# Masks of two block-masked attentions: from matmuls of their own to extra contraction rows of q and k

## The chip, the cores and the metric

The kernel runs on one NeuronCore of a Trainium2 chip. Its time is the device time of one execution in microseconds (us). Three runs of the kernel before gave 829.72, 831.28 and 831.41 us; the median is 831.28.

## What is computed

Two layers of a streaming encoder, on 256 tokens (four chunks of 64) of width 1024, all in float32:

```python
for l in range(2):
    u = rms_norm(x, g_mix_pre)
    qa, ka, va, cq, ckv, ga, gb = split(u @ w_in)        # 1024, 128, 128, 384, 288, 1024, 1024 columns
    # A: 16 query heads in 2 groups of 8, 2 key heads, 64 wide, rotary;
    #    a query of chunk c sees the keys of chunks c-1 and c; a learned sink in the softmax's sum
    y_a = swa_sink_attention(rope(qa), rope(ka), va, sinks)
    # B: 8 heads, 96 wide (64 + 32 rotary), from low-rank latents;
    #    a query of chunk c sees the keys of chunks 0 .. c
    y_b = mla_attention(q(rms_norm(cq) @ w_uq), kv(rms_norm(c_kv) @ w_ukv, k_pe))
    m = sigmoid(ga + b0) * (y_a @ w_oa) + sigmoid(gb + b1) * (y_b @ w_ob)
    x = x + rms_norm(m @ w_out)
    x = x + rms_norm(relu(rms_norm(x) @ w_mlp_in)**2 @ w_mlp_out)
```

Both masks are by whole chunks: a score outside the allowed chunks is set to -1e30 before the softmax.

## The kernel before

Each engine has a program of its own, written out by hand in order, and they meet at semaphores. Nothing is scheduled: an engine that waits holds up all that stands behind it. Tokens lie in two tiles of 128 (t = 0, 1).

*Weights.* A weight piece is loaded by SyncE (`raw`), cast on ScalarE to its high part (`hi`, L582, buffer `w_hi`) and subtracted on VectorE to its low part (`lo`, L853, `w_lo`). A product then takes three matmuls (high times high, low times high, high times low: L1166 to L1168). The activations, turned by TensorE (L1143, bank `tp`), are split in the same way (`s_hi` on ScalarE L605 or L602, `s_lo` on VectorE L883 or L880).

*Attention.* Queries and keys are float32 and are not split. They are turned by TensorE into `tp`, four blocks of 128 columns a fill, and copied by VectorE (`turned_copy`) into `qT_a`, `kT_a`, `qT_b`, `kT_b`. For A the two groups share the partitions: group 0 lies at partitions 0 to 63 and group 1 at 64 to 127 of `qT_a` and `kT_a`, and `q_of_group` writes the queries into `tok` with the two groups interleaved by head, so that a block of 128 columns holds a head of either group.

The scores are worked off in 18 quanta (`QUANTA`): four of A at t = 0 with four heads of 128 keys; eight of A at t = 1 with two heads of 192 keys; two of B at t = 0 with four heads of 128 keys; four of B at t = 1 with two heads of 256 keys. For each quantum `scores` (L1250) issues one float32 matmul a head, which the trace shows as two passes, and then one more matmul (L1251) with two stationary rows of ones (`chunk_of`) and two rows of 0 and -1e30 (`mask`), which adds the mask to all heads of the quantum in the score bank.

Step i of 20 on TensorE (L1343 on): the scores of quantum i, the turned probabilities of quantum i-2 (`turn_probs`), one piece of the gate or output product (12 matmuls of 512 columns), the values of quantum i-2 (`values`, L1282), then what `EXTRA` lists for this step: a fill of q, k or finished y. VectorE takes the row maxima of each quantum (L942), copies the turned blocks, and splits a weight piece; ScalarE takes the exponentials (L669).

*Start.* GpSimdE builds constants before the layers: the frequencies, the identity, then `chunk_of` and `mask` (L451 to L461, 12 memsets, most of 64 columns on one partition), then the cosine table (L466 to L468). The constants are done at 5.9 us of the profiled execution and the table at 7.1. Only then come its reciprocal roots of the sums of squares (`to_rstd`, L476 and L480; the first two from 19.66 to 21.5), for which VectorE waits before it scales the first projection (L1041). Meanwhile VectorE works out the angles (L822 to L837, one after the other, each waited for), ScalarE waits for them with the sines (L563), the first instruction of its program, and then turns to the first `s_hi` and `w_hi`.

## Time and profile before

| | |
|---|---|
| time, median of three runs | 831.28 us |
| the profiled execution | 827.3 us from its first to its last instruction; no separate time is listed for it, the median of the runs is 4.0 us above its span |
| PE busy | 803.6 us, 97% |
| DVE / ACT / POOL busy | 511.2 / 407.9 / 124.4 us |
| DMA | 132.35 MB, mean 160 GB/s |
| score matmuls (L1250) | 192 passes: 128 of A, 64 of B; 4% of the chain |
| mask matmuls (L1251) | 36 |

PE, DVE, ACT, POOL and SP are TensorE, VectorE, ScalarE, GpSimdE and SyncE; PEld is TensorE's weight load. A busy PE is not a PE at its peak: matmuls overlap, each row's duration holds its way through the array, so what a matmul costs is read from the distance between the starts of neighbours. A bracket at a row's end is the engine's idle time before it and who ended it.

### The profile page before, as it was taken

How to read it: one execution, taken by the hardware profiler on the slowest of the kernel's cores; microseconds unless marked ns; L12 is line 12 of the kernel's file. 1: busy time of each engine (PE TensorE's matmuls, PEld its weight loads, DVE VectorE, ACT ScalarE, POOL GpSimd, SP SyncE). 2: the span in 40 equal slices, each digit the busy share in tenths (PEclk: the TensorE clock that was granted, in tenths of full speed). 3: DMA queues.
4: the chain of work that ended last, by engine and by line, in shares of the span. 5: the costliest groups of instructions: out<-in, count | busy, mean ns of one | idle time of the engine just before them, and what ended most of it. 6: DMA issues, size and time to landing. Idle time of an engine off the chain costs nothing.

```text
span 827.3 us, 13460 instructions
## 1 busy us (share of the span) xinstructions
PE 803.6 (97%) x4613; PEld 696.0 (84%) x4613; DVE 511.2 (62%) x685; ACT 407.9 (49%) x747; POOL 124.4 (15%) x204
## 2 busy tenths in 40 slices
PE   6999999999999999999979999999999999999997
PEld 5987877888779999999869888788878899999995
DVE  5767666566785545554567777666666854555554
ACT  6756434444474444444466574434345644454452
POOL 2443000001231000000015420000031200000000
PEclk9999999999999999999989999999999999999999
DMA  7647422334646555556328382321436555565521
GB/s 236 237 167 266 154 82 72 103 105 150 204 131 226 172 185 183 175 200 191 98 56 284 138 304 93 102 93 62 153 113 213 184 191 175 194 194 172 192 102 51
DMA packets 68476, 132.35 MB, mean 160 GB/s; under 512 B 2842, under 2 KB 10564, under 8 KB 68164
## 3 DMA queue, kind: packets, MB, share of 16 engines
q1 hardware_dynamic: 68276, 131.12, 47.6%
q8 instruction: 30, 0.49, 0.2%
q10 hardware_dynamic: 144, 0.52, 0.2%
q14 instruction: 26, 0.21, 0.1%
HBM read 130.59 MB, written 1.05 MB: 159 GB/s over the span
## 4 chain that ended last, share of the span: by engine, by line
PE 91%; DVE 4%; ACT 2%; issue 2%; DMA 1%; SPq 0%; ACTq 0%; POOL 0%; DVEq 0%; POOLq 0%
PE acc L1166 17%; PE acc L1167 17%; PE acc L1168 17%; PE sc L1416 6%; PE sc L1415 6%; PE sc L1414 6%; PE tp L1143 5%; PE acc L1282 5%; PE sc L1250 4%; PE acc L1200 4%; DVE w_lo L853 1%; ACT s_hi L605 1%; PE sc L1166 1%; PE sc L1168 1%; PE sc L1167 1%
## 5 line engine op out<-in xcount | busy, mean ns | idle before, releaser
L853 DVE TENSOR_TENSOR w_lo<-raw,w_hi 128x1024 fp32r<-128x1024 f32 (+3 forms) x256 | 311.9, 1234 | 192.1 <-ACT w_hi L582 187.1
L582 ACT CAST w_hi<-raw 128x1024 fp32r<-128x1024 f32 (+3 forms) x256 | 252.3, 996 | 215.1 <-PE acc L1168 143.9
L1166 PE MATMUL acc<-w_hi,s_hi 128*128 128x512 f32 (+3 forms) x680 | 262.9, 387 | 3.7 <-DVE w_lo L853 3.7
L1167 PE MATMUL acc<-w_lo,s_hi 128*128 128x512 f32 (+3 forms) x680 | 257.5, 379 | 0.0
L1168 PE MATMUL acc<-w_hi,s_lo 128*128 128x512 f32 (+3 forms) x680 | 257.5, 379 | 0.0
L1166 PEld LDWEIGHTS acc<-w_hi,s_hi 128*128 128x128 f32 x680 | 127.9, 188 | 28.0 <-DVE w_lo L853 5.6
L1168 PEld LDWEIGHTS acc<-w_hi,s_lo 128*128 128x128 f32 x680 | 127.8, 188 | 23.9
L1167 PEld LDWEIGHTS acc<-w_lo,s_hi 128*128 128x128 f32 x680 | 128.1, 188 | 21.0
L1414 PE MATMUL sc<-s_hi,w_hi 128*128 128x256 f32 x448 | 126.9, 283 | 0.0
L1416 PE MATMUL sc<-s_hi,w_lo 128*128 128x256 f32 x448 | 126.8, 283 | 0.0
L1415 PE MATMUL sc<-s_lo,w_hi 128*128 128x256 f32 x448 | 126.8, 283 | 0.0
L1414 PEld LDWEIGHTS sc<-s_hi,w_hi 128*128 128x128 f32 x448 | 85.9, 192 | 0.7
L1415 PEld LDWEIGHTS sc<-s_lo,w_hi 128*128 128x128 f32 x448 | 85.9, 192 | 0.5
L1416 PEld LDWEIGHTS sc<-s_hi,w_lo 128*128 128x128 f32 x448 | 85.9, 192 | 0.0
L493 POOL TENSOR_TENSOR tok<-k_b 128x512 f32<-128x512 f32 x32 | 36.4, 1159 | 266.5 <-ACT k_b L650 266.5
L669 ACT ACTIVATE probs<-sc,neg_m 128x128 f32<-128x128 f32 (+2 forms) x96 | 37.6, 402 | 49.6 <-DVE neg_m L945 34.8
L537 POOL TENSOR_TENSOR tok<-gate_a,gate_b 128x512 f32<-128x512 f32 x8 | 14.1, 1782 | 261.0 <-DVE gate_b L993 261.0
L602 ACT ACTIVATE s_hi<-tp 128x512 fp32r<-128x512 f32 x24 | 13.7, 596 | 48.4 <-PE tp L1143 48.4
L942 DVE TENSOR_REDUCE row_max<-sc 128x2 f32<-128x384 f32 (+2 forms) x36 | 22.6, 627 | 13.3 <-PE sc L1251 13.3
L605 ACT ACTIVATE s_hi<-tp,gain 128x128 fp32r<-128x128 f32 x76 | 21.1, 379 | 17.0 <-PE tp L1143 15.0
L650 ACT ACTIVATE k_b<-sc 128x512 f32<-128x512 f32 x28 | 15.2, 595 | 25.7 <-PE sc L1416 25.7
L1200 PE MATMUL acc<-w_hi,s_hi 128*128 128x384 f32 (+1 forms) x64 | 19.7, 429 | 7.5 <-ACT w_hi L582 6.8
(143 smaller groups left out, 778.4 us busy)
## 6 DMA issues: line engine op xcount, KB each, us to landing
raw<-in_w_mlp_in SPq DMA_DIRECT2D x32, 1024.0 KB, 5.3
raw<-in_w_mlp_out SPq DMA_DIRECT2D x32, 1024.0 KB, 5.0
raw<-in_w_in SPq DMA_DIRECT2D x24, 1024.0 KB, 6.4
raw<-in_w_oa SPq DMA_DIRECT2D x8, 1024.0 KB, 5.0
raw<-in_w_out SPq DMA_DIRECT2D x8, 1024.0 KB, 5.0
raw<-in_w_ob SPq DMA_DIRECT2D x4, 1024.0 KB, 5.0
raw<-in_w_in SPq DMA_DIRECT2D x4, 768.0 KB, 4.6
raw<-in_w_in SPq DMA_DIRECT2D x4, 576.0 KB, 6.1
```

What stands on the lines that cost most here:

```text
L582: s.copy(split_view(w_hi, p), raw_view(p)).then_inc(hi_ready, 1)
L669: ins = s.activation(probs[:, i % 2, a * w + skip:(a + 1) * w], sc[i % 2][:, a * w + skip:(a + 1) * w], ACT.Exp, bias=neg_m[:, c + a:c + a ...
L853: v.tensor_tensor(split_view(w_lo, p), raw_view(p), split_view(w_hi, p).bitcast(F32), ALU.subtract)\
L1143: ins = nc.tensor.transpose(b[0:rows, i * P:(i + 1) * P], src, ident[:, :])
L1166: mm(banks[t][:, 0:N], h[:, kk, tk], wh[:, k, :], start=(start and k == 0), stop=False)
L1167: mm(banks[t][:, 0:N], h[:, kk, tk], wl[:, k, :], start=False, stop=False)
L1168: ins = mm(banks[t][:, 0:N], low[:, kk, tk], wh[:, k, :], start=False, stop=(stop and k == b - a - 1))
L1200: ins = mm(acc[t][:, 0:N], xs[:, 2 * i + k, t * P:(t + 1) * P], w[:, k, :], start=(first and i == 0 and k == 0), stop=(last and i == 3 and ...
L1282: ins = mm(y[:, (h + a) * 64:(h + a + 1) * 64], pt, vv, start=(b == 0), stop=(b == w // P - 1))
L1414: mm(out, wh[:, k, cols], s1_hi[:, kk, :], start=(i == 0 and k == 0 and f % 2 == 0), stop=False)
L1415: mm(out, wh[:, k, cols], s1_lo[:, kk, :], start=False, stop=False)
L1416: ins = mm(out, wl[:, k, cols], s1_hi[:, kk, :], start=False, stop=(i == 3 and k == 1 and f % 2 == 1))
```

## The change

The mask matmul and its two constant tiles are gone. The turned tiles get extra rows: `qT_a` and `kT_a` have 66 rows (64 and one for each of the tile's two chunks), `qT_b` and `kT_b` have 100 (96 and one for each of the four chunks). The extra rows of q say in ones which chunk a query is of; those of k hold -1e30 where a query of that chunk may not see the key. They are written once, before the layers, by GpSimdE: 15 instructions (`chunk_rows`), a memset and two affine selects for each of five regions. `qT_a` now holds one token tile and 16 heads, all at partitions 0 to 63, so a block of 128 columns that is turned holds two heads of one group, and the odd heads are copied from partitions 64 to 127 down to 0 to 63: a fill of q takes two copies of half the partitions, and the fill of k takes four (two groups, and the 192 keys of tile 1 are stored apart from the 128 of tile 0). `tok` holds the queries in their natural order. In `EXTRA` the fill `("qA", 1, 1)` moves from step 2 to step 3 and the fills of B are reordered (q before k), the last one going to step 11.

```diff
 SCALE_B = BQK ** -0.5
+NCHUNK = SEQ // CHUNK
+AK, BK = AD + P // CHUNK, BQK + NCHUNK
+A_KEYS = (slice(0, P), slice(CHUNK, SEQ))
+A_AT = (slice(0, P), slice(P, P + SEQ - CHUNK))
 NGAIN = KD + KD + KQ + KV
...
 NQ = len(QUANTA)
+CONST_STEPS = 15
 NSTEP = NQ + 2
...
-EXTRA = {1: [("qA", 1, 0)], 2: [("qA", 1, 1)],
-         3: [("kB", 0, 0)], 4: [("qB", 0, 0)], 5: [("kB", 0, 1)], 6: [("qB", 0, 1), ("y", 0)],
-         7: [("kB", 1, 0)], 8: [("qB", 1, 0), ("y", 1)], 9: [("kB", 1, 1)], 10: [("qB", 1, 1)],
+EXTRA = {1: [("qA", 1, 0)], 3: [("qA", 1, 1)],
+         4: [("qB", 0, 0)], 5: [("kB", 0, 0)], 6: [("qB", 0, 1), ("y", 0)], 7: [("kB", 0, 1)],
+         8: [("qB", 1, 0), ("y", 1)], 9: [("qB", 1, 1)], 10: [("kB", 1, 0)], 11: [("kB", 1, 1)],
          12: [("y", 2)], 15: [("y", 3)], 18: [("y", 4)]}
...
         v_b = sb("v_b", [P, TT, BH * BV])
-        qT_a = sb("qT_a", [P, AG, SEQ])
-        kT_a = sb("kT_a", [P, SEQ])
-        qT_b = sb("qT_b", [BQK, BH, SEQ])
-        kT_b = sb("kT_b", [BQK, BH, SEQ])
+        qT_a = sb("qT_a", [AK, AH, P])
+        kT_a = sb("kT_a", [AK, AKV, A_AT[1].stop])
+        qT_b = sb("qT_b", [BK, BH, SEQ])
+        kT_b = sb("kT_b", [BK, BH, SEQ])
         probs = sb("probs", [P, 2, COL])
...
         ident = sb("ident", [P, P])
-        chunk_of = sb("chunk_of", [P, P], F32R)
-        mask = sb("mask", [P, 3, 2 * P], F32R)
         pos_i = sb("pos_i", [P, TT], I32)
...
-            return tok[:, t, :].rearrange("p (h g d) -> p g h d", g=AKV, h=AG)[:, g, :, :]
+            return tok[:, t, g * COL:(g + 1) * COL].rearrange("p (h d) -> p h d", h=AG)
...
-            sel, mk = chunk_of[:, :].bitcast(F32), mask[:, :, :].bitcast(F32)
-            steps.link(g.memset(sel, 0.0))
-            steps.link(g.memset(mk, 0.0))
-            for half in range(2):
-                r = 2 * 32 * half
-                steps.link(g.memset(sel[r:r + 1, 0:CHUNK], 1.0))
-                steps.link(g.memset(sel[r + 32:r + 33, CHUNK:P], 1.0))
-
-                steps.link(g.memset(mk[r:r + 1, 0, CHUNK:P], NEG))
-                steps.link(g.memset(mk[r:r + 1, 1:3, P + CHUNK:2 * P], NEG))
-
-                g.memset(mk[r + 32:r + 33, 1, CHUNK:P], NEG).then_inc(consts_ready, 1)
-                pool.wait_ge(consts_ready, half + 1)
+            consts = Steps(pool, consts_ready)
+
+            def chunk_rows(view, low, high, inside, outside):
+
+                _, heads, n = view.shape
+                consts.link(g.memset(view, inside))
+                consts.link(g.affine_select(
+                    out=view, in_=view, compare_op=ALU.is_ge, fill=outside, base=-CHUNK * low,
+                    pattern=[[0, heads], [1, n]], channel_multiplier=-CHUNK))
+                consts.link(g.affine_select(
+                    out=view, in_=view, compare_op=ALU.is_ge, fill=outside, base=CHUNK * (high + 1) - 1,
+                    pattern=[[0, heads], [-1, n]], channel_multiplier=CHUNK))
+
+            chunk_rows(qT_a[AD:AK, :, :], 0, 0, 1.0, 0.0)
+            chunk_rows(qT_b[BQK:BK, :, :], 0, 0, 1.0, 0.0)
+            chunk_rows(kT_a[AD:AK, :, A_AT[0]], -1, 0, 0.0, NEG)
+            chunk_rows(kT_a[AD:AK, :, A_AT[1]], 0, 1, 0.0, NEG)
+            chunk_rows(kT_b[BQK:BK, :, :], 1 - NCHUNK, 0, 0.0, NEG)
+            assert consts.n == CONST_STEPS
...
                 if name[0] == "kA":
-                    ins = v.tensor_copy(kT_a[:, :], b[:, 0:SEQ])
+                    for g in range(AKV):
+                        for t in range(TT):
+                            ins = v.tensor_copy(kT_a[0:AD, g, A_AT[t]], b[g * AD:(g + 1) * AD, A_KEYS[t]])
                 elif name[0] == "qA":
-                    _, t, h = name
-                    ins = v.tensor_copy(qT_a[:, 4 * h:4 * h + 4, t * P:(t + 1) * P],
-                                        b[:, :].rearrange("p (h n) -> p h n", h=4))
+                    _, t, g = name
+                    for odd in range(2):
+                        ins = v.tensor_copy(qT_a[0:AD, g * AG + odd:(g + 1) * AG:2, :],
+                                            b[odd * AD:(odd + 1) * AD, :].rearrange("p (h n) -> p h n", h=AG // 2))
                 elif name[0] in ("qB", "kB"):
...
                     dst = qT_b if name[0] == "qB" else kT_b
-                    ins = v.tensor_copy(dst[:, 4 * h:4 * h + 4, t * P:(t + 1) * P],
+                    ins = v.tensor_copy(dst[0:BQK, 4 * h:4 * h + 4, t * P:(t + 1) * P],
                                         b[0:BQK, :].rearrange("p (h n) -> p h n", h=4))
...
                     pe.wait_ge(probs_ready, pos.count(NQ, i - 1))
-                r0, r1 = (64 * g, 64 * g + 64) if kind == "A" else (0, P)
-                which = 0 if t == 0 else (1 if kind == "A" else 2)
                 b = sc[i % 2]
-
-                k0 = w // P - 1 if kind == "B" else 0
-                nk = w // P - k0
-                view = b[:, :].rearrange("p (h k c) -> p h k c", h=n, c=P)[:, :, k0:, CHUNK:P]
-                mk = mask[r0:r1, which, 0:w].rearrange("p (k c) -> p k c", c=P)[:, k0:, CHUNK:P]\
-                    .unsqueeze(1).to_broadcast([r1 - r0, n, nk, CHUNK])
                 for a in range(n):
                     if kind == "A":
-                        q = qT_a[r0:r1, h + a, t * P:(t + 1) * P]
-                        k = kT_a[r0:r1, skip:w]
+                        q = qT_a[:, g * AG + h + a, :]
+                        k = kT_a[:, g, A_AT[t]]
                     else:
...
                         k = kT_b[:, h + a, 0:w]
-                    mm(b[:, a * w + skip:(a + 1) * w], q, k, start=(a == 0), stop=False)
-                mm(view, chunk_of[r0:r1, :], mk, start=False, stop=True).then_inc(scores_ready, 1)
+                    ins = mm(b[:, a * w + skip:(a + 1) * w], q, k, start=(a == 0), stop=(a == n - 1))
+                ins.then_inc(scores_ready, 1)
...
                     _, t, h = name
-                    blocks = [tok[:, t, (4 * h + a) * AKV * AD:(4 * h + a + 1) * AKV * AD] for a in range(4)]
+                    blocks = [tok[:, t, (4 * h + a) * 2 * AD:(4 * h + a + 1) * 2 * AD] for a in range(4)]
                 elif name[0] in ("qB", "kB"):
...
                 turned(pos, ("qA", 0, 1))
-                pe.wait_ge(consts_ready, 2)
+                pe.wait_ge(consts_ready, CONST_STEPS)
                 for i in range(NSTEP):
...
                     for name in EXTRA.get(i, []):
-                        if i in (1, 3):
+                        if i in (1, 4):
```

TensorE, step 4 of a layer: the fill before it, the scores of the first quantum of A at t = 1, the turned probabilities and the first product matmuls. Before:

```order
L1143 MATMUL tp<-ident,k_b 96x128 x4
L1233 REGISTER_ALU
L1250 MATMUL sc<-kT_a,qT_a 128x192 x2
L1251 MATMUL sc<-mask,chunk_of 128x4x64
L1143 MATMUL tp<-ident,probs 128x128 x4
L1157 REGISTER_ALU
L1306 ISA
L1166 MATMUL acc<-w_hi,s_hi 128x512
```

After:

```order
L1155 MATMUL tp<-ident,tok 128x128 x4
L1245 REGISTER_ALU
L1254 MATMUL sc<-kT_a,qT_a 128x192 x2
L1155 MATMUL tp<-ident,probs 128x128 x4
L1169 REGISTER_ALU
L1310 ISA
L1178 MATMUL acc<-w_hi,s_hi 128x512
```

The mask matmul has gone from between the scores and the turned probabilities, and another fill stands ahead.

GpSimdE, the end of the constants and the cosine table behind them. Before:

```order
L455 MEMSET chunk_of 1x64
L456 MEMSET chunk_of 1x64
L458 MEMSET mask 1x64
L459 MEMSET mask 1x2x64
L461 MEMSET mask 1x64
L466 TENSOR_TENSOR cost<-turns 128x64
L467 TENSOR_SCALAR cost<-cost 128x64
L468 TENSOR_SCALAR sint<-sint 128x2x32
```

After:

```order
L458 MEMSET kT_a 2x2x192
L459 AFFINE_SELECT kT_a<-kT_a 2x2x192
L462 AFFINE_SELECT kT_a<-kT_a 2x2x192
L458 MEMSET kT_b 4x2048
L459 AFFINE_SELECT kT_b<-kT_b 4x2048
L462 AFFINE_SELECT kT_b<-kT_b 4x2048
L475 TENSOR_TENSOR cost<-turns 128x64
L476 TENSOR_SCALAR cost<-cost 128x64
L477 TENSOR_SCALAR sint<-sint 128x2x32
```

Ahead of the first row shown stand six more memsets before the change, and nine more instructions after it (the same three for `qT_a` and for `qT_b` over 2048 columns, and for `kT_a` over 2x128). All fifteen stand ahead of the cosine table and of the roots.

VectorE, the copies of turned A blocks ahead of the first scores (`tp` is the bank, L1061 and L1073 the sinks). Before:

```order
L853 TENSOR_TENSOR w_lo<-raw,w_hi 128x512
L898 ISA
L901 COPY kT_a<-tp 128x256
L898 REGISTER_ALU
L904 COPY qT_a<-tp 128x4x128
L898 REGISTER_ALU
L904 COPY qT_a<-tp 128x4x128
L1060 ISA
L1061 TENSOR_SCALAR neg_sink<-sink_in 128x16
```

After:

```order
L862 TENSOR_TENSOR w_lo<-raw,w_hi 128x512
L907 ISA
L912 COPY kT_a<-tp 64x128
L912 COPY kT_a<-tp 64x192
L912 COPY kT_a<-tp 64x128
L912 COPY kT_a<-tp 64x192
L907 REGISTER_ALU
L916 COPY qT_a<-tp 64x4x128 x2
L907 REGISTER_ALU
L916 COPY qT_a<-tp 64x4x128 x2
L1072 ISA
L1073 TENSOR_SCALAR neg_sink<-sink_in 128x16
```

One copy of k has become four, and each copy of q two.

## Rows read from the trace of the kernel before

**Rows 1.** The page, part 4: the chain that ended last, by engine.
```profile
PE 91%; DVE 4%; ACT 2%; issue 2%; DMA 1%; SPq 0%; ACTq 0%; POOL 0%; DVEq 0%; POOLq 0%
```

**Rows 2.** Stretch of one layer's attention: busy us (count), granted clock, DMA share, GB/s.
```profile
70.00:180.00 110.00, 110.00 (x628) 91.26 (x627) 72.59 (x125) 52.85 (x143) 2.38 (x3) 1.00 0.39 130
```

**Rows 3.** PE timeline, quantum of A, t = 0: start us, us, instructions.
```profile
80.42 0.60 PE L1143 MATMUL tp<-ident,tok 128*128 128x128 f32 x4
80.94 1.16 PE L1250 MATMUL sc<-kT_a,qT_a 64*128 64x128 f32 x8
...
82.56 0.48 PE L1166 MATMUL acc<-w_hi,s_hi 128*128 128x512 f32 x1
```

**Rows 4.** PE timeline, quantum of B, t = 0.
```profile
147.04 0.61 PE L1143 MATMUL tp<-ident,tok 128*128 128x128 f32 x4
147.49 1.06 PE L1250 MATMUL sc<-kT_b,qT_b 96*128 96x128 f32 x8
148.30 0.36 PE L1251 MATMUL sc<-mask,chunk_of 128*128 128x256 f32 x1
148.50 0.60 PE L1143 MATMUL tp<-ident,probs 128*128 128x128 f32 x4
148.86 0.48 PE L1166 MATMUL acc<-w_hi,s_hi 128*128 128x512 f32 x1
```

**Rows 5.** PE timeline, quantum of A, t = 1.
```profile
92.08 0.60 PE L1143 MATMUL tp<-ident,k_b 128*96 128x128 f32 x4
...
93.98 0.48 PE L1166 MATMUL acc<-w_hi,s_hi 128*128 128x512 f32 x1
```

**Rows 6.** PE timeline, quantum of B, t = 1.
```profile
163.15 0.61 PE L1143 MATMUL tp<-ident,tok 128*128 128x128 f32 x4
163.59 1.03 PE L1250 MATMUL sc<-kT_b,qT_b 96*128 96x256 f32 x4
164.27 0.41 PE L1251 MATMUL sc<-mask,chunk_of 128*128 128x128 f32 x1
164.52 0.60 PE L1143 MATMUL tp<-ident,probs 128*128 128x128 f32 x4
164.88 0.48 PE L1166 MATMUL acc<-w_hi,s_hi 128*128 128x512 f32 x1
```

**Rows 7.** DVE groups by shape: busy us, mean ns, idle before.
```profile
L904 DVE COPY qT_a<-tp 128x512 f32<-128x512 f32 x8 | 5.5, 691 | 4.9 <-PE tp L1143 4.8
...
L901 DVE COPY kT_a<-tp 128x256 f32<-128x256 f32 x2 | 0.8, 424 | 0.9 <-PE tp L1143 0.9
```

**Rows 8.** POOL timeline, start of the program.
```profile
2.21 0.29 POOL L442 TENSOR_SCALAR_AFFINE_SELECT ident<-ident 128x128 f32<-128x128 f32 x1 [0.25 <-POOL ident L441]
...
3.05 0.74 POOL L452 MEMSET mask<- 128x768 f32 x1
3.85 0.14 POOL L455 MEMSET chunk_of<- 1x64 f32 x1
...
19.66 0.19 POOL L476 TENSOR_TENSOR var<-sums,norm_k 128x1 f32<-128x1 f32 x1 [12.59 <-ACT squares L612]
```

**Rows 9.** DVE timeline, start of the program.
```profile
3.14 0.71 DVE L824 TENSOR_SCALAR ang<-freq,pos_f 128x32 f32<-128x32 f32 x2
...
5.11 0.19 DVE L837 TENSOR_SCALAR ang<-ang 128x64 f32<-128x64 f32 x1
...
23.23 1.13 DVE L1041 TENSOR_SCALAR latent<-acc,rstd 128x384 f32<-128x384 f32 x2
```

**Rows 10.** ACT timeline, start of the program.
```profile
7.18 1.12 ACT L605 ACTIVATE s_hi<-tp,gain 128x128 fp32r<-128x128 f32 x4
...
11.91 1.56 ACT L582 CAST w_hi<-raw 128x768 fp32r<-128x768 f32 x2 [0.80 <-DMA raw<-in_w_in]
```

**Rows 11.** POOL timeline, rotation of the queries.
```profile
58.91 1.30 POOL L335 TENSOR_TENSOR gate_a<-tok,sint 128x512 f32<-128x512 f32 x1 [7.06 <-ACT tok L710]
```

**Rows 12.** DVE timeline, the same stretch.
```profile
59.01 1.75 DVE L336 TENSOR_TENSOR tok<-tok,cost 128x512 f32<-128x512 f32 x1
```

## The prediction

> **What bounds the kernel.** I read the chain that ended last first: TensorE holds 91% of it, and no other engine more than 4% [rows 1]. The stretch of the attention, where most of the change lies, says the same: TensorE is busy for all of 110 us at full clock, VectorE for 73, ScalarE for 53, GpSimdE for 2, and the DMA engines for 39% [rows 2]. So in this stretch a matmul that goes is worth the distance that it held between its neighbours' starts, and nobody else ends the waits. The same stretch comes once more in the second layer. The second place to read is the start of the program, before the layers: there TensorE has nothing to do yet, and a chain over GpSimdE, VectorE and ScalarE decides when it begins [rows 8 to 10].
>
> **TensorE: the quanta of the attention.** I compare passages from the first of the four turns ahead of the scores to the first product matmul behind them.
>
> A at t = 0: 80.42 to 82.56, 2.14 us [rows 3]. B at t = 0 has the same counts and columns, but its q and k fill 96 partitions instead of 64: 147.04 to 148.86, 1.82 us [rows 4]. The 0.32 between them is the price of 64-row operands among 128-row ones; the first part of it is seen ahead of the scores, where four turns hold 0.52 us in front of A and 0.45 in front of B. With 66 rows I take A to behave as B with its 96. The mask itself: in B the passes stand 0.11 apart (147.49 to 148.30, eight passes and 0.03), and from the last of them to the turned probabilities it is 0.03 + 0.20 = 0.23, where 0.11 would stand without the mask: 0.12. So A at t = 0 gives 0.32 + 0.12 = 0.44.
>
> A at t = 1: 92.08 to 93.98, 1.90 us [rows 5]. B at t = 1: 163.15 to 164.88, 1.73 us, with passes of 256 columns 0.217 apart (163.59 to 164.27, less 0.03, by three) [rows 6]. With 192 columns a pass would be 0.163, and four of them 0.22 less: 1.51. Difference 0.39. The mask of B at t = 1: 0.03 + 0.25 - 0.217 = 0.065. So A at t = 1 gives 0.455.
>
> The Trainium skill, page "TensorEngine Tiling (Array Packing)", Key Properties, says that a change of tiling mode drains TensorE, and counts a contraction of up to 64 as its own mode. By that rule the 66-row operands stay in the full mode, which is what the 0.52 against 0.45 points to; without the rule only the masks would go (rival C).
>
> Per layer: 4 x 0.44 + 8 x 0.455 + 2 x 0.12 + 4 x 0.065 = 5.9; two layers 11.8 us. The first two quanta of a layer have no turned probabilities behind them; I price them alike. The rest of the moved work has one answer: the same 64 turns of q and k are issued, a fill has gone from step 2 to 3 and one from 10 to 11, and nobody waits for them closely. The extra contraction rows cost no time of their own: B's passes with 96 rows and the turns with 128 (147.04 to 147.49, four) both stand 0.11 apart [rows 4].
>
> **VectorE: the copies.** 512 columns take 0.691, 256 take 0.424 [rows 7]: 1.04 ns a column and 0.16 fixed. A fill of q goes from 0.69 to two of 0.42, which overlap a little; VectorE is busy for two thirds of the attention [rows 2], which hides it. The fill of k goes from 0.42 to two of 0.29 and two of 0.36, 1.3 in sum. Here something waits: TensorE's third fill needs the bank that the k fill leaves, and VectorE sits idle for the k fill to come (0.9 in two [rows 7]), so what is added lies on the path. Between 0.5 (full overlap of the fixed parts) and 0.9; I take 0.7 a layer, 1.4 in both. Left on TensorE: 11.8 - 1.4 = 10.4 us gained.
>
> **GpSimdE: the constants.** This is paid once. A memset of 768 columns takes 0.74, of 64 columns 0.14: 0.85 ns a column, so 2048 columns take 1.84 us. An affine select of 128 columns takes 0.29 [rows 8]. With the fixed part of a GpSimdE instruction that reads (0.19 for one column [rows 8]) that is 0.82 ns a column and 1.9 us for 2048; with the memset's fixed part (0.09) it is 1.57 ns and 3.3 us. I take 1.9, since a select reads. Three memsets of 1.84, six selects of 1.9, six small instructions of together 2.5, and 15 gaps of 0.06 make 20.5 us, from 2.8 to 23.3, where the old constants ended at 5.9 (the kernel before, *Start*, which has the other ends that I use).
>
> Two paths wait behind that. *The roots.* The cosine table (1.1 us) and two roots (0.85 each) follow: 26.1. VectorE needed them at 23.23 [rows 9], so by this path alone the start is 2.8 us late. *The port.* In the trace a VectorE instruction that both reads and writes SBUF does not run beside one of GpSimdE. Its first two angle steps, 32 columns each, take 0.71 together and end at 3.85, just behind GpSimdE's mask memset, which ran from 3.05 to 3.79 [rows 8, 9]. At 59.01 a rotation step takes 1.75 while GpSimdE runs from 58.91 to 60.21 [rows 11, 12]. So it stands until the other's instruction is over, and with instructions of 1.9 instead of 0.14 every step of the angle chain can cost one of them. Seven steps in a row follow each other by semaphores. GpSimdE's next instruction started 0.06 after its memset had ended (3.79 to 3.85), when VectorE's held steps had only just ended, so I take GpSimdE to be first each time. The first steps end with the first memset at 4.6, the six others behind the next five large instructions and a small one: 14.8. They ended at 5.3 (5.11 + 0.19 [rows 9]): 9.5 us later, and ScalarE's first split of x, 1.9 behind them [rows 10], as well. It then no longer waits for its first weights (0.8 in [rows 10] and a little before): 8.6. Last, VectorE's splits of the first four weight pieces, which read and write SBUF too, meet the last three large instructions: one more of them, about 2. Together 10.6 us late, with which the roots are long ready. Nothing catches it up, since TensorE bounds what follows.
>
> The Trainium skill, "GPSIMD Engine Reference", Key points, says that GpSimdE shares its SBUF interfaces with VectorE, in conflict with instructions that have two SBUF inputs or run in a two-port mode; the angle steps in the trace have been seen to be held.
>
> **Sum.** The profiled execution: 827.3 - 10.4 + 10.6 = 827.5 us of span, with 4.0 around it as in the median of the runs before: 831.5 us against 831.28. No change that can be measured (a measurement tells 0.2%, 1.7 us).
>
> **Rivals.**
>
> *A, faster.* VectorE slips in between two of GpSimdE's instructions. The small steps ran among memsets of 0.14 with 0.19 each, without a sign of being held, and GpSimdE's lead at each meeting is some hundredths of a microsecond. If every second step slips in, the angles are ready at some 10.7 and the start is 5 to 7 late; if rows on two or four partitions hold no port at all, only the roots count, 2.8. I take 5.5: 831.3 - 10.4 + 5.5 = 826.4 us. Against it: the first two steps were plainly held.
>
> *B, slower.* The affine selects are slower than 1.9 us, by the column or by the row of heads in their pattern, which the one select of the trace doesn't show. With 3.3 the angles wait for four selects more dearly (5.6 us) and the splits for one (1.4): 17.6 late, 838.5 us; it decides from about 2.2 us on. With 2.6 it is 835.0. I take 836. Against it: fixed parts of reading instructions are 0.19 in the trace. The skill's "GPSIMD Engine Reference", section 3.1, gives 1.03 cycles an element for a light body and 1.8 for the best ordinary loop; as an estimate from its 1.2 GHz, the second makes 3.1 us and speaks for this rival.
>
> *C, the change doesn't do what it says for A's operands.* The 66 rows switch as dearly as the 64 did, and only the masks go: about 24 x 0.12 + 4 x 0.12 + 8 x 0.065 = 3.9, less 1.4. With the start: 831.3 - 2.5 + 10.6 = 839.4 us. Against it: the 96 rows of B, which are no full height either, show no such step.
>
> **How the numbers follow.** My forecast 0.37, A 0.34, B 0.25, C 0.04. The forecast's own range is 829 to 834 (its start between 8.5 and 13), of which 0.06 lies more than 0.2% below and 0.07 as far above. Faster: 0.34 + 0.06 = 0.40. Slower: 0.25 + 0.04 + 0.07 = 0.36. The same: 0.24. The range reaches into A to 824.5 (roots only would be 823.7) and into B to 838.
>
> **What the profile after would show.** Score passages of A of 1.7 us at t = 0 and 1.45 at t = 1 instead of 2.14 and 1.90, with 0.44 for the four turns ahead; if they stay at 2.0, C holds. The first attention stretch shorter by 5.9 and the wait for the k copies longer by 0.7. GpSimdE's nine long instructions of 1.9 each: if the selects take over 2.2, B. The last angle step at 14.8 and the first `s_hi` at 16.7: if they come at 11 or earlier, A. VectorE's first scaled projection near 34 instead of 23.2. I am wrong in the main thing if the start is not late at all.

## The result: 0.36% slower, and the profile after

| | before | after |
|---|---|---|
| median, six runs of each on one chip | 830.5 us (829.54 to 831.41) | 833.09 us (832.35 to 833.65) |
| ratio, 95% interval | | 1.0036 [1.0025, 1.0047] |
| span of the profiled execution | 827.3 us | 831.9 us |
| from the turn of k to the last turned y, either layer | 112.37, 112.35 us | 108.59, 108.60 us |
| start of the turn of k, first layer | 65.22 us | 77.44 us |

The time lies in the forecast's range, 1.6 us above the value. But the forecast was 0.2 us slower than before, no change that can be measured, and 0.36% is more than the 0.2% that I had called the least that a measurement tells: in kind this is the outcome "slower", to which I had given 0.36. The two lower lines are read from starts on TensorE (`tp<-ident,kv_a` is the turn of k; the last turned y lies in `latent`); they carry the whole story. The attention gained 3.77 us a layer where 5.2 were forecast, and the start lost 12.2 where 10.6 were forecast. What lies between the two stretches and behind the second is alike in these two profiles (296.61 and 296.55; 240.73 in both).

The chain that ended last, by engine; it answers to [rows 1]:

```profile
PE 88%; DVE 7%; issue 2%; ACT 2%; DMA 0%; ACTq 0%; DVEq 0%; POOL 0%; POOLq 0%
```

VectorE has gone from 4 to 7%. Twelve microseconds later in the program than [rows 2], the stretch of the attention:

```profile
82.00:192.00 110.00, 109.34 (x634) 92.83 (x633) 78.29 (x135) 54.30 (x145) 3.58 (x2) 1.00 0.40 132
```

TensorE is no longer busy without a gap, and VectorE is busy for 78 us instead of 73. GpSimdE's start, which answers to [rows 8]:

```profile
2.85 1.80 POOL L458 MEMSET qT_a<- 2x2048 f32 x1
4.72 2.00 POOL L459 TENSOR_SCALAR_AFFINE_SELECT qT_a<-qT_a 2x2048 f32<-2x2048 f32 x1
6.79 2.00 POOL L462 TENSOR_SCALAR_AFFINE_SELECT qT_a<-qT_a 2x2048 f32<-2x2048 f32 x1
8.85 1.80 POOL L458 MEMSET qT_b<- 4x2048 f32 x1
...
22.03 2.47 POOL L462 TENSOR_SCALAR_AFFINE_SELECT kT_b<-kT_b 4x2048 f32<-4x2048 f32 x1
```

Memsets of 1.80 and, but for the last, selects of 1.94 to 2.00, as forecast (1.84, 1.9). VectorE beside them, against [rows 9]:

```profile
3.02 1.66 DVE L831 CAST pos_f<-pos_i 128x2 f32<-128x2 int32 x1 [3.02 <-DMA pos_i<-in_positions]
4.71 2.19 DVE L833 TENSOR_SCALAR ang<-freq,pos_f 128x32 f32<-128x32 f32 x2
6.94 1.91 DVE L841 TENSOR_SCALAR turns<-ang 128x64 f32<-128x64 f32 x1
8.88 1.82 DVE L842 TENSOR_SCALAR turns<-turns 128x64 f32<-128x64 f32 x1
10.74 4.27 DVE L844 SCALAR_TENSOR_TENSOR ang<-turns,ang 128x64 f32<-128x64 f32 x3
15.04 0.19 DVE L846 TENSOR_SCALAR ang<-ang 128x64 f32<-128x64 f32 x1
```

Compare the ends: 4.68 against GpSimdE's 4.65, 8.85 against 8.79, 10.70 against 10.65. Six of the nine steps end 0.03 to 0.08 us behind the long one beside them. The other three are short and were not held: the second one of L833 (0.23, in the gap that began at 6.72), the last one of L844 (0.22, beside a memset of 0.30) and L846. The angles are ready at 15.2 (forecast 14.8), the first scaled projection comes at 35.48 (forecast near 34).

Not every meeting holds VectorE, though. Its first split of a weight piece, with two inputs in SBUF, took its ordinary 0.96 beside a memset, and its second 1.95, held by the select that had begun at 19.94:

```profile
17.99 1.80 POOL L458 MEMSET kT_b<- 4x2048 f32 x1
18.98 0.96 DVE L862 TENSOR_TENSOR w_lo<-raw,w_hi 128x768 fp32r<-128x768 f32 x1 [3.08 <-ACT w_hi L591]
```

On TensorE a quantum of A at t = 0, one of A at t = 1 and one of B at t = 0 (of the last two the first and last line), against [rows 3 to 5]:

```profile
93.11 0.60 PE L1155 MATMUL tp<-ident,tok 128*128 128x128 f32 x4
93.55 1.06 PE L1254 MATMUL sc<-kT_a,qT_a 66*128 66x128 f32 x8
94.44 0.60 PE L1155 MATMUL tp<-ident,probs 128*128 128x128 f32 x4
94.80 0.48 PE L1178 MATMUL acc<-w_hi,s_hi 128*128 128x512 f32 x1
...
103.47 0.61 PE L1155 MATMUL tp<-ident,tok 128*128 128x128 f32 x4
...
104.93 0.48 PE L1178 MATMUL acc<-w_hi,s_hi 128*128 128x512 f32 x1
...
155.75 0.61 PE L1155 MATMUL tp<-ident,tok 128*128 128x128 f32 x4
...
157.44 0.48 PE L1178 MATMUL acc<-w_hi,s_hi 128*128 128x512 f32 x1
```

A at t = 0 holds 1.69 us (it was 2.14), A at t = 1 holds 1.46 (1.90), B at t = 0 holds 1.69 (1.82): 0.45, 0.44 and 0.13 less, as forecast, and 0.44 stands ahead of the scores of A. So TensorE was handed its gain. Who took it back stands in the waits of TensorE from just ahead of the turn of k to the end of the first layer's attention (who waited for whom, us in total, times, longest), before and then after:

```profile
PE acc L1166 <- DVE w_lo L853: 1.3, 1, 1.3
```

```profile
PE acc L1178 <- DVE w_lo L862: 1.5, 2, 1.3
PE tp L1155 <- DVE kT_a L912: 0.8, 1, 0.8
PE acc L1286 <- DVE probsT L932: 0.5, 1, 0.5
```

All of them are VectorE's. The wait of 1.3 falls ahead of the turn of k in both (its matmul starts at 64.07 before) and is outside the stretch; the other 1.5 us of the kernel after are new. VectorE's rows at the first fills and in step 4:

```profile
77.86 1.13 DVE L912 COPY kT_a<-tp 64x128 f32<-64x128 f32 x4 [0.43 <-PE tp L1155]
79.02 2.81 DVE L916 COPY qT_a<-tp 64x512 f32<-64x512 f32 x4
...
105.47 1.38 DVE L916 COPY qT_a<-tp 64x512 f32<-64x512 f32 x2
106.89 0.56 DVE L954 TENSOR_REDUCE row_max<-sc 128x2 f32<-128x384 f32 x1
...
107.65 0.69 DVE L932 COPY probsT<-tp 128x512 f32<-128x512 f32 x1
```

A q copy of 64 partitions has 512 columns and takes 0.69, exactly what one of 128 partitions took [rows 7]. I had put 0.42. Four of them stand ahead of the weight piece that the first score step multiplies with, and two in step 4 stand ahead of the row maxima and of `probsT`, for which the values wait (the 0.5 above).

### The profile page after: what moved, and what is told of

Read it like the earlier page. It is cut to its first block, busy times and chain, and to the rows that moved or that the text cites. A ratio compares the mean times of both kernels' runs of the same rounds, so it can differ in the third digit from the quotient of the medians.

```text
span 831.9 us, 13410 instructions
## 1 busy us (share of the span) xinstructions
PE 795.3 (96%) x4577; PEld 693.2 (83%) x4577; DVE 526.2 (63%) x699; ACT 407.3 (49%) x747; POOL 145.2 (17%) x207
## 4 chain that ended last, share of the span: by engine, by line
PE 88%; DVE 7%; issue 2%; ACT 2%; DMA 0%; ACTq 0%; DVEq 0%; POOL 0%; POOLq 0%
PE acc L1178 17%; PE acc L1180 16%; PE acc L1179 16%; PE sc L1420 6%; PE sc L1419 6%; PE sc L1418 6%; PE acc L1286 5%; PE tp L1155 4%; PE acc L1212 4%; PE sc L1254 3%; DVE w_lo L862 2%; ACT s_hi L614 1%; PE sc L1178 1%; PE sc L1180 1%; PE sc L1179 1%
## 5 line engine op out<-in xcount | busy, mean ns | idle before, releaser
L1178 PEld LDWEIGHTS acc<-w_hi,s_hi 128*128 128x128 f32 x680 | 127.9, 188 | 29.1 <-DVE w_lo L862 5.6
L546 POOL TENSOR_TENSOR tok<-gate_a,gate_b 128x512 f32<-128x512 f32 x8 | 14.1, 1782 | 251.7 <-DVE gate_b L1005 251.7
L1212 PEld LDWEIGHTS acc<-w_hi,s_hi 128*128 128x128 f32 x64 | 12.9, 221 | 22.9 <-ACT w_hi L591 19.5
L954 DVE TENSOR_REDUCE row_max<-sc 128x2 f32<-128x384 f32 (+2 forms) x36 | 22.6, 627 | 11.6 <-PE sc L1254 11.4
```

What stands on the lines that cost most here:

```text
L1178: mm(banks[t][:, 0:N], h[:, kk, tk], wh[:, k, :], start=(start and k == 0), stop=False)
L1212: ins = mm(acc[t][:, 0:N], xs[:, 2 * i + k, t * P:(t + 1) * P], w[:, k, :], start=(first and i == 0 and k == 0), stop=(last and i == 3 and ...
```

## The experiments

Each was timed in five rounds beside the kernel before, in three sessions, where the median of before was 830.17, 830.15 and 830.88 us. All times are medians; all carry a ratio to before of the same session with its interval. "The stretch" is the one from the turn of k to the last turned y, 112.37 before and 108.59 after.

### The constants alone

```diff
+            chunk_rows(qT_b[BQK:BQK + 2, :, :].rearrange("p h (c n) -> p (h c) n", n=P), 0, 0, 1.0, 0.0)
+            chunk_rows(qT_b[BQK:BK, :, :], 0, 0, 1.0, 0.0)
+            chunk_rows(qT_b[BQK:BQK + 2, 0:2, 0:P], -1, 0, 0.0, NEG)
+            chunk_rows(qT_b[BQK:BQK + 2, 0:2, 0:192], 0, 1, 0.0, NEG)
+            chunk_rows(kT_b[BQK:BK, :, :], 1 - NCHUNK, 0, 0.0, NEG)
```

> The kernel before, with one thing added: the 15 instructions of chunk_rows on GpSimdE, of the same shapes, behind the old mask constants, into rows that nobody reads. Nothing in the attention changes. Theory (VectorE is held, each of its steps for one whole instruction of GpSimdE, even if that writes two or four partitions): the angles are ready near 15 to 16, the first s_hi near 17 to 18, VectorE's first scaled projection near 35 to 36, and the kernel is 12 to 13 us slower than before, 843. Rival (rows on so few partitions hold nobody, only the roots behind the constants come late): 2.8 to 4 us slower, 834. Second rival (the start is caught up later, behind a TensorE that had slack): under 2 us.

Measured: 840.58 us, 1.0122 [1.0107, 1.0137], 10.4 slower. The size is near the theory's 12 to 13, the way is not. Written behind the old mask constants, the long instructions came too late to meet the angle chain:

```profile
5.20 0.20 DVE L860 TENSOR_SCALAR ang<-ang 128x64 f32<-128x64 f32 x1
...
15.54 4.51 DVE L876 TENSOR_TENSOR w_lo<-raw,w_hi 128x768 fp32r<-128x768 f32 x2
...
32.42 1.14 DVE L1064 TENSOR_SCALAR latent<-acc,rstd 128x384 f32<-128x384 f32 x2 [4.99 <-POOL rstd L503]
```

```profile
6.05 1.80 POOL L473 MEMSET qT_b<- 2x2048 f32 x1
...
10.00 2.73 POOL L477 TENSOR_SCALAR_AFFINE_SELECT qT_b<-qT_b 2x2048 f32<-2x2048 f32 x1
...
30.66 0.19 POOL L499 TENSOR_TENSOR var<-sums,norm_k 128x1 f32<-128x1 f32 x1 [0.25 <-POOL sint L491]
```

The angles were done at 5.4, then VectorE's splits were held instead (two took 4.51, where they took 1.81), GpSimdE's selects were held in turn (2.73 instead of 2.0), and the roots came 11 us late (30.66 against 19.66), so VectorE waited 4.99 for them. The holding goes both ways. The clock adds to it: TensorE stood idle for 6 us behind the late roots, and the stretch after that reads a granted clock of 0.50 (the figure behind the counts), where its passes of 288 columns stood 0.24 apart instead of 0.13:

```profile
34.80:41.50 6.70, 5.88 (x26) 5.89 (x27) 4.08 (x7) 3.02 (x9) 2.46 (x5) 0.50 0.69 229
```

From the first scaled projection to the turn of k it took 44.2 us here and 42.0 before. So some 2.2 of the 11.4 us by which the start is late came by a way that the kernel after doesn't have, and that the sum is near 12 is luck.

So I moved the same instructions ahead of the old constants, where the change has them.

> The kernel before, with the 15 long GpSimdE instructions of the change ahead of its old mask constants, at the place in the program where the change has them; nobody reads what they write. In the run with them behind the old ones VectorE's angle steps had all slipped by before the first long one began (the last at 5.20, the first long memset at 6.05), and only the roots came late (31.2). Theory: now the angle chain meets them as in the kernel after: angles at 15, first s_hi at 17 to 18, and the whole is 12 to 14 us slower than before (the old constants and the table come on top): 843. Rival (the start costs what the roots cost, in whichever order): 10.4 again, 840.6.

Measured: 841.1 us, 1.0132 [1.0115, 1.0149], 10.95 slower. Its angle steps are those of the kernel after to 0.02 us; the last one (15.04 there):

```profile
15.05 0.20 DVE L861 TENSOR_SCALAR ang<-ang 128x64 f32<-128x64 f32 x1
```

The turn of k stands at 76.63, the stretch is 112.38. The expected whole was 843. By the time alone the rival's 840.6 is nearer; the trace decides for the theory, since here the angle chain is held and no roots are waited for, as in the kernel after. Its span is 12.1 us longer than before's, its median only 10.95; the difference is treated under "Span and median" below. The constants alone cost 11 us, and nothing of it is caught up.

### The constants behind the cosine table

```diff
-            chunk_rows(qT_a[AD:AK, :, :], 0, 0, 1.0, 0.0)
-            chunk_rows(qT_b[BQK:BK, :, :], 0, 0, 1.0, 0.0)
...
             g.tensor_scalar(sint[:, :, 0, :], sint[:, :, 1, :], -1.0, None, ALU.mult).then_inc(tables_ready, 1)
             pool.wait_ge(tables_ready, 1)
+            chunk_rows(qT_a[AD:AK, :, :], 0, 0, 1.0, 0.0)
+            chunk_rows(qT_b[BQK:BK, :, :], 0, 0, 1.0, 0.0)
...
```

> The kernel after, with the 15 long GpSimdE instructions behind the cosine table instead of ahead of it. The angle chain meets none of them; they now end near 25 and lie beside VectorE's first splits, and ahead of the roots. Theory (each VectorE instruction on SBUF is held for one whole instruction of GpSimdE, and the roots come late): the start is late by the roots, 3 to 4 us beyond 23.2, and by held splits, 2 to 5 more: 6 to 9 late instead of 12.2, 827 to 830. Rival (only the roots count, in both orders): no difference from after, 833.

Measured: 832.53 us, 1.0029 [1.0019, 1.0040]; after had 1.0036. The rival's number, for another reason than the rival's. The angle chain is free, but:

```profile
9.46 4.74 DVE L863 TENSOR_TENSOR w_lo<-raw,w_hi 128x768 fp32r<-128x768 f32 x2 [3.06 <-ACT w_hi L592]
...
32.66 1.14 DVE L1054 TENSOR_SCALAR latent<-acc,rstd 128x384 f32<-128x384 f32 x2 [3.82 <-POOL rstd L490]
```

Some 20 us of GpSimdE, drawn out to 24 by VectorE's own instructions (6.83 to 30.65), stand ahead of roots that were wanted at 19.66. As with the constants alone, TensorE idled (5 us) behind them, and 34.1 to 40.8 reads a granted clock of 0.50. Moving the block trades one victim for the other. My 3 to 4 us for the roots had left out two things: that the block is drawn out, and that it begins later (6.83).

### Small patterns

```diff
+            chunk_rows(pat_q[:, :, :], 0, 0, 1.0, 0.0)
+            chunk_rows(pat_b[:, :, :], 1 - NCHUNK, 0, 0.0, NEG)
+            chunk_rows(pat_a[:, :, A_AT[0]], -1, 0, 0.0, NEG)
+            chunk_rows(pat_a[:, :, A_AT[1]], 0, 1, 0.0, NEG)
...
+                pool.dma_start(dst, src.unsqueeze(1).to_broadcast([src.shape[0], heads, n])).then_inc(rows_ready, 16)
```

> The kernel after, with the constants made once for one head (12 GpSimdE instructions of at most 320 columns) and spread over the heads by four DMAs on GpSimdE's queue. The attention is that of the kernel after. Theory: nearly all of the 12.2 us by which the start is late goes, with twelve short instructions of 0.1 to 0.4 us left: angles near 6 to 7 instead of 15.2, the time 11 to 12 us below after, 821.5. Rival (the start matters only through the roots): 9 to 10 us, 823.5, or, if the DMAs delay the first weight pieces by as much as they save, 826.

Measured: 823.32 us, 0.9912 [0.9896, 0.9928]: 9.8 below after, and now clearly faster than before. The stretch is 108.58, the same as after's. The angles are ready at 5.6 us instead of 15.2. The time is the rival's 823.5, but not by the rival's way: in the kernel after VectorE's first scaled projection (35.48) waited for no root, so it was the held steps that this run gave back. The 11 to 12 us were too many; what is missing stands under "TensorE at the start".

### Who copies the turned blocks

```diff
-                    for odd in range(2):
-                        ins = v.tensor_copy(qT_a[0:AD, g * AG + odd:(g + 1) * AG:2, :],
-                                            b[odd * AD:(odd + 1) * AD, :].rearrange("p (h n) -> p h n", h=AG // 2))
+                    ins = v.tensor_copy(qT_a[0:AD, g * AG:(g + 1) * AG:2, :],
+                                        b[0:AD, :].rearrange("p (h n) -> p h n", h=AG // 2))
...
+                    ins = s.activation(qT_a[0:AD, g * AG + 1:(g + 1) * AG:2, :],
+                                       b[AD:P, :].rearrange("p (h n) -> p h n", h=AG // 2), ACT.Copy)
```

and in the same way for the second group of k.

> As the kernel with small patterns, and the copies of the turned A blocks shared: VectorE copies the half at partitions 0 to 63, ScalarE the half at 64 to 127, for k and for all four fills of q. Theory (a copy costs by its columns, so halving the partitions had doubled what a fill costs on VectorE: 0.70 us a layer at k, 0.45 at the first q and 0.72 in step 4): up to 1.87 a layer, 3.7 in both, comes back: 817.5 to 819. Rival (VectorE had room, the waits lie elsewhere): no difference from the small patterns, 821.5. Second rival (ScalarE's exponentials and casts come late by its copies): slower than the small patterns by 1 to 3 us.

Measured: 819.45 us, 0.9869 [0.9854, 0.9884], 3.9 below the small patterns (the 817.5 to 819 expected started from 821.5, which those missed). The stretch is 106.89: 1.69 a layer or 3.4 in both come back by it, within the 3.7 expected. The one wait of TensorE that is left in it:

```profile
PE tp L1188 <- DVE kT_a L944: 0.3, 1, 0.3
```

Next, only the q copies shared:

> The kernel with small patterns, and of its copies of turned blocks only those of A's queries are shared (VectorE the half at partitions 0 to 63, ScalarE the other); the four k copies stay on VectorE. Theory (the q copies, which the prediction took as hidden, cost 0.45 a layer ahead of the scores and 0.72 in step 4; the k copies the rest): 2 x 1.2 = 2.4 us below the small patterns, 820.9, and 1.4 us above the kernel with all copies shared, 819.45. Rival (the k copies cost all of it and the q copies were hidden as the prediction had it): no difference from the small patterns, 823.3.

Measured: 820.37 us, 0.9875 [0.9860, 0.9890], in another session than the other two. By the stretch, which does not depend on the start: 107.41, so q is worth 1.17 a layer and k 0.52. The rival is out. Laid side by side with the small patterns, pass by pass, TensorE gains 0.44 at the weight piece ahead of the first scores (71.69 there) and 0.73 at the values of step 4 (97.44 there), and nothing elsewhere. The q copies cost 2.3 us in both layers. Whether it is the second copy alone or also its place is open: the change moves the fill `("qA", 1, 1)` from step 2 to 3, and no run leaves it where it was.

### What TensorE gained from

```diff
-                        q = qT_a[:, g * AG + h + a, :]
-                        k = kT_a[:, g, A_AT[t]]
+                        q = qT_a[0:AD, g * AG + h + a, :]
+                        k = kT_a[0:AD, g, A_AT[t]]
```

> The kernel after, with the scores of A contracted over 64 rows instead of 66 (A's mask is left out of the scores; everything else stands). No instruction more or less, no column more or less. Theory (what A gained beyond its masks came from the height of the operands, 0.32 a quantum at t = 0 and 0.39 at t = 1): 2 x (4 x 0.32 + 8 x 0.39) = 8.8 us slower than after, 842. Rival (the gain came from the masks gone and from all heads lying at partition 0): no difference from after, 833.

Measured: 839.31 us, 1.0111 [1.0094, 1.0128], 6.2 above after; the stretch is 112.03, 3.44 longer. The quantum to compare with 93.11 to 94.80 of after:

```profile
93.11 0.60 PE L1155 MATMUL tp<-ident,tok 128*128 128x128 f32 x4
93.63 1.16 PE L1254 MATMUL sc<-kT_a,qT_a 64*128 64x128 f32 x8
94.72 0.66 PE L1155 MATMUL tp<-ident,probs 128*128 128x128 f32 x4
95.13 0.48 PE L1178 MATMUL acc<-w_hi,s_hi 128*128 128x512 f32 x1
```

The same counts and columns, two rows less, and 0.33 us more: 0.08 ahead of the scores, 0.20 from the first score pass to the turned probabilities, 0.05 from these to the product. Lying at partition 0 gave nothing: this passage takes 2.02 us, and the one of the kernel without masks below, where A still lies at partitions 0 and 64, takes 2.03. The first quantum pays only 0.10, and in step 4 the price of 0.34 hides behind the wait for `probsT`; the rest makes the 3.44 measured. The rows are worth 0.33 at t = 1 as well; the 0.39 that this run's theory took for them still held 0.06 of A's larger mask.

The other part, from the kernel before:

```diff
-                    mm(b[:, a * w + skip:(a + 1) * w], q, k, start=(a == 0), stop=False)
-                mm(view, chunk_of[r0:r1, :], mk, start=False, stop=True).then_inc(scores_ready, 1)
+                    ins = mm(b[:, a * w + skip:(a + 1) * w], q, k, start=(a == 0), stop=(a == n - 1))
+                ins.then_inc(scores_ready, 1)
```

> The kernel before, without the 36 mask matmuls (the masks are left out of both attentions; A still lies at partitions 0 to 63 and 64 to 127 with 64 rows). Theory (the masks themselves are the smaller part of what TensorE gained, and the 64 rows the larger): 24 x 0.12 + 4 x 0.12 + 8 x 0.065 = 3.9 us faster than before, 826.3, and the passages of A still hold their 0.52 ahead of the scores. With 0.33 a quantum from the run with 64 rows (7.9 in both layers), masks and rows would then be 11.8, against 11.35 by the marks. Rival (the mask matmul, which sat between operands of 64 and of 128 rows, was what switched, and without it the switch goes too): 8 us or more, 822.

Measured: 826.4 us, 0.9946 [0.9932, 0.9960], 4.5 faster; the stretch is 110.53, 1.83 a layer, 3.7 in both. A quantum of A at t = 0:

```profile
81.07 0.60 PE L1143 MATMUL tp<-ident,tok 128*128 128x128 f32 x4
81.60 1.16 PE L1250 MATMUL sc<-kT_a,qT_a 64*128 64x128 f32 x8
...
83.10 0.48 PE L1166 MATMUL acc<-w_hi,s_hi 128*128 128x512 f32 x1
```

2.03 us; 2.14 less the 0.12 of the mask was the sum. The 0.53 ahead of the scores stays, as the theory had it. The masks are a third of TensorE's gain, and the height of the operands is the rest.

### TensorE at the start

The kernel with small patterns still reached the turn of k 1.3 us later than before (66.50 against 65.22). Its passes of 384 columns stood 0.32 apart until 16.6 us, those of before until 14.1. The same start in the kernel with only the q copies shared reached the turn of k at 65.35, so most of that is a matter of the single execution. First I moved the patterns behind the table, then I kept TensorE at work.

> As the kernel with small patterns and shared copies, the 12 short instructions behind the cosine table. Theory (short instructions cost VectorE's angle chain 0.3 us, which this gives back; they end near 12, long before the roots): 0.3 to 0.5 us below 819.4. Rival (TensorE's passes stand at twice their distance at the start, 0.32 for 384 columns until 16.5 us where before it was until 13.5, for a reason of its own): no more than 0.3 in either direction, 819.4.

Measured: 819.24 us, 0.9871 [0.9855, 0.9888]. Inconclusive: not told apart from the 819.45 of the patterns ahead of the table.

```diff
+            def spin(n):
+
+                for i in range(n):
+                    nc.tensor.transpose(sc[1][:, (i % 4) * P:(i % 4 + 1) * P], ident[:, :], ident[:, :])
...
+                if kind == "x":
+                    spin(14)
```

> As the kernel with the patterns behind the table, and TensorE turns the identity into a score bank that nobody reads, 11 times while it has nothing to do at the start and 14 times between the turns of x and the first product of each layer. Theory (the 1.2 us that the start of the kernel with small patterns is late lies in TensorE's passes of 384 columns, 0.32 apart, which is the lower of the two clocks, until 16.5 us; an engine that has worked right before runs at the higher one): the first passes are 0.16 apart from the start, and 1 to 2 us come back in each layer: 815 to 817.5. Rival (the distance comes from operands or banks, not from the clock): no gain, or 1 us of loss by the extra turns.

Measured: 818.7 us, 0.9861 [0.9844, 0.9877]: half a microsecond, not told apart from none, and outside the 815 to 817.5 expected. Its first products in the first layer, those in the second, and the stretch behind these:

```profile
7.13 1.69 PE L1186 MATMUL sc<-ident 128*128 128x128 f32 x14
9.52 0.62 PE L1253 MATMUL acc<-w_hi,s_hi 128*128 128x384 f32 x2 [0.69 <-ACT w_hi L605]
...
412.09 0.62 PE L1253 MATMUL acc<-w_hi,s_hi 128*128 128x384 f32 x2 [2.34 <-ACT w_hi L605]
413.85 1.01 PE L1253 MATMUL acc<-w_hi,s_hi 128*128 128x384 f32 x2 [1.14 <-ACT w_hi L605]
```

```profile
412.90:419.60 6.70, 5.75 (x16) 4.80 (x17) 5.63 (x12) 2.36 (x4) 0.00 (x0) 0.50 0.28 79
```

Two passes hold 0.62 after the extra turns, where they hold 1.01 without them (9.58 in the small patterns); so the distance follows from what the engine did before, and the theory's mechanism stands. Yet the gain does not come. In the first layer the passes stay 0.17 to 0.18 apart from the first one on, but then TensorE waits for weight pieces instead, and the turn of k comes at 65.34 instead of 65.62. In the second layer TensorE idles for 2.3 us behind the extra turns, and from 412.9 on the granted clock reads 0.50 and the passes are 0.32 apart once more; the way from the first layer's last turned y to the second's turn of k, 297.27 us, is no shorter than the 296.28 without the extra turns.

## Why the prediction came out as it did

**TensorE's gain: mechanism right, 0.2 a layer too large.** Forecast 5.9 a layer. The kernel with shared copies is 5.48 shorter (112.37 to 106.89) and still waits 0.20 more for k than before, so the gain is 5.7; the passages of the eighteen quanta, added up, give 5.72. Per quantum it is 0.45 at t = 0 and 0.45 at t = 1, against 0.44 and 0.455 forecast. What is missing is the first quantum, which gives 0.20: I had priced the first two like the others. Masks are 1.83 of it (forecast 1.94), rows of A the rest. Rival C is dead: 66 rows behave as 96 do.

**The k copies: right.** Forecast 0.7 a layer. TensorE's third fill starts 1.06 us behind the last turn ahead of it instead of 0.35, which is 0.71; sharing took back 0.5 of it.

**The q copies: the step that failed.** "A fill of q goes from 0.69 to two of 0.42 [...] which hides it". Two errors in one. 512 columns on 64 partitions are still 512 columns: 0.69 each, not 0.42 (the order of the change shows them: `64x4x128 x2`). And "busy for two thirds" is a mean over the stretch. At two places of each layer VectorE is just in time, ahead of the first scores and in step 4, and what is added there reaches TensorE: 0.44 and 0.73 us. That a fill went from step 2 to 3 and "nobody waits for them closely" did not hold in the second place either. Measured 1.17 a layer, 2.3 us, forecast nothing. Without it the change would have come out near 830.8.

**The start: right in kind, about right in size.** Forecast 10.6; the constants alone cost 10.95 by medians, 12.1 by the spans. Some steps within it differed. The first CAST of positions, on two columns, was held too (1.66), which I had not counted, and two later steps were not held, which made up for it: that the angles came within 0.4 of the forecast is in part luck. The prediction's rule, that a VectorE instruction which reads and writes SBUF does not run beside one of GpSimdE, was too wide: the splits were held by selects and not by memsets. And TensorE's passes stood at the larger distance from 19.0 to 29.0, 10 us, where before it was 9.4 to 14.1. GpSimdE won each meeting with a long instruction in the angle chain, once with both starts within 0.01 us, and rival A (every second step slips in) is dead: the one step that slipped in between two long instructions came right behind another in the same gap. Rival B's selects of 2.2 or more did not come but for one of 2.47, which waited for VectorE. The parts of the constants add up to 20.3, not 20.5; they took 21.65 (2.85 to 24.50).

The sum by parts: 10.95 - 2 x 3.77 = 3.4 us slower; measured 833.09 - 830.5 = 2.6, or 3.0 by the ratio. The forecast had 10.6 - 10.4 = 0.2. Of the difference, 2 x 1.42 lies in the attention: 1.17 of q and 0.2 of the gain, with nothing for k. That the time fell into the range shows its width (5 us) as much as the mechanism: a term of 2.3 us was missing from it.

**Span and median.** The spans differ by 4.6 us and the medians by 2.6. In every execution for which both are on record the time is 1.7 to 1.9 us above the span. So the profiled execution of before took about 829.1 us (an estimate: 827.3 and 1.8), as short as the shortest on record (829.09, of 829.09 to 831.52), while that of the kernel after took 833.65, the longest of its six. Part of the reason shows at the start. The kernel without masks has the same program up to there. Before, then that one:

```profile
14.31 1.59 PE L1200 MATMUL acc<-w_hi,s_lo 128*128 128x384 f32 x8
15.74 1.04 PE L1143 MATMUL tp<-ident,x 128*128 128x128 f32 x8
```

```profile
14.64 2.15 PE L1200 MATMUL acc<-w_hi,s_lo 128*128 128x384 f32 x8
16.63 1.04 PE L1143 MATMUL tp<-ident,x 128*128 128x128 f32 x8
```

TensorE's passes came closer together at 14.1 us in the one execution and at 15.9 in the other, and the turns of x stand 0.9 us apart. The way between the two layers varies too, from 296.3 to 297.6 us over the twelve profiles. What the prediction called 4.0 "around" the span was some 2 us of the luck of its profile; as it used the same 4.0 for both kernels, its difference was not touched.

**The better version.** Small patterns and shared copies together, 819.24 to 819.45 us (818.7 with the extra turns), beat both kernels: 1.3% below before, 1.6% below after. The idea of the change was worth 11 us; its constants and its copies had eaten it.

## What to carry to other kernels

Price a copy or an elementwise step by its columns on each partition: two copies of half the partitions cost twice what one of all costs (0.69 us each here). A mean busy share is no proof that added work is hidden; look at the rows around the moment when the bound engine needs the result, and if the neighbour is just in time there, the added work costs its full length. Constants are work on the path when what they delay is on it, here VectorE's angle chain or the roots, wherever the block stood: build them once, small, and spread them by DMA.

## What the runs showed of the hardware

- A GpSimdE instruction on two or four partitions can hold VectorE for its whole length. VectorE's step of 64 columns (0.19) lasts as long as the select beside it (1.9), and the select is drawn out (2.0 to 2.73) by VectorE's splits. The Trainium skill, "GPSIMD Engine Reference", Key points, names conflicts with VectorE instructions that have two SBUF inputs or a two-port mode. Here `turns<-ang`, with one input, and a CAST of two columns were held; whether they ran in a two-port mode no run shows.
- Which instructions meet matters. Steps with one tensor input (CAST, `turns<-turns`, the copy of `gain`) were held by memsets too (1.66, 1.82 and, with the constants alone, 1.72 us). Those with two SBUF inputs were held by selects and not by memsets: beside a memset of 1.8 a split took its ordinary 0.96 (18.98 in the kernel after) and 0.76 (23.56 with the constants alone), beside a select up to 2.75.
- Operands of 64 rows among 128-row ones cost 0.33 us a passage against 66 rows, and all of it stands at the two edges. From the last turn to the first score pass of 64 rows it is 0.20, from that to the second 0.21, then 0.11 six times, then 0.20 to the first turned probabilities and 0.16 to the second. With 66 rows all of these are 0.11. The Trainium skill, "TensorEngine Tiling (Array Packing)", Key Properties, has the rule; its size here is 0.33.
- TensorE's passes of 384 columns stood 0.32 us apart in the first microseconds of work (1.2 GHz) and 0.16 later (2.4 GHz), while the granted clock in the profile's stretches reads 1.00 for both. That holds for the start of the program alone. Later the reading follows the distance: 416.9 to 423.5 of before, behind an idle time of 3.5 us and with passes 0.32 apart, reads 0.50, and so do the stretches behind the late roots (34.8 to 41.5 with the constants alone, 34.1 to 40.8 with them behind the table). When they changed over at the start differed by some 2 us between executions of the same start.
